# FFN-in linears of a two-block transformer kernel: the high weights against both activation halves in one 512-column matmul

## Chip, cores and metric

One core of a Trainium2 chip runs the whole program. The metric is the device time of one execution in microseconds.

## The reference

Two stacked blocks on a sequence of 256 tokens with width 1024 in float32. The first block has two layers, and each layer has two SwiGLU feed-forward nets (four in all), with an attention between them:

```
mod = c_act @ ada_w[layer] + ada_b[layer]
h = modulate(rms_norm(x, norm_g[layer, 0]), sh1, sc1)
x = x + 0.5 * g1[:, None, :] * swiglu(h, ffn_w_in[layer, 0], ffn_w_out[layer, 0])
```

`swiglu` multiplies h by a matrix of 1024 x 5632, takes silu of one half of the result times the other half, and multiplies that (hidden width 2816) by a matrix of 2816 x 1024. The modulation vectors `mod` come from matrices of their own, 1024 x 9216 a layer. The second block has convolution mixers, a cross attention and a gather of expert rows (PEER).

## The kernel before, in words

**Three matmuls for one product.** TensorE works on float32r operands. To keep float32 accuracy every weight tile and every activation is split into a high half and a low half, and a product is high x high + high x low + low x high. For a block of 128 output features and each of 8 input chunks k, `product` (L801) issues three matmuls of 256 columns (the tokens) into one PSUM bank: w_hi with HH, w_hi with HL, w_lo with HH. HH and HL are the activation's halves; the linears of f01_in read EH and EL.

**Weight tiles.** A weight tile is 1024 x 256, 1 MB, two blocks of 128 features. SP loads it into `raw`, a ring of three (L610; it waits until the low half of the tile three before has been made, L601). ScalarE copies it to `w_hi` (`split`, L1302: it waits for the load and for TensorE's end of the tile three before). VectorE makes `w_lo` = raw - w_hi (`split`, L1865). TensorE waits for the low half of a tile (L810) before the tile.

**An FFN.** The in-stage (f00_in, f01_in, f10_in, f11_in) has 22 tiles; the two blocks of tile t are the gate and the up half of hidden chunk t. ScalarE takes Silu of the first from PSUM (L1422), VectorE multiplies it by the second from PSUM (L1986) into `graw`, ScalarE copies that to `GUH` (high half, L1425) and GpSimd subtracts to `GUL` (low half, L711). The out-stage has 16 tiles of 1408 columns of weights, two for each of 8 feature blocks: 33 matmuls each. The first out-tile waits for hidden chunks 0 to 10, the second for all 22 (`hidden_lo`, L933).

**Order of work.** Each engine's program is written out by hand, slot by slot (a slot is one tile), with semaphores between them. 18 tiles of an in-stage are a loop of three passes over six tiles, the last ones are written out. In f01_in and f11_in the first two tiles are done ahead by another path (`raw_tile`), so that the loop begins at tile 2. The first tile of the stage waits for the activation's halves chunk by chunk; in `feat_tile` this is the branch `new` (L825 to L841), and since the branch is taken by the slot's number inside the loop, it is run in each of the three passes. The rest of the tiles take `product`.

**What shares the engines.** In f00, f01 and f10 VectorE also computes the modulation vectors (`mod_tile`, L1872: two scalar_tensor_tensor of 1024 with an accumulator over a 1 MB tile in `mod_ring`, a ring of two): in the in-stage in slots 0, 1, 3 and 4 of each six and in the last slots (18 to 21 counted from the loop's first tile, as far as they exist), then once per feature block of the out-stage. ScalarE's queue issues their loads (`load_mod`, L1316 and on), each after the tile two before has been eaten. f11 has no modulation tiles.

The slot of VectorE before: modulation tile, split of tile t+2, multiply of tile t. The slot of ScalarE before: load of a modulation tile, Silu of t, GUH copy of t, split of tile t+3. PSUM has six banks in turn for the outputs, three tiles.

## Time and profile before

| | us |
|---|---|
| median of 3 runs | 2137.27 |
| lowest, highest | 2137.02, 2140.35 |
| profiled execution, span | 2138.9 |
| TensorE busy (matmuls) | 1807.5, 85% |
| TensorE weight loads | 1552.8, 73% |
| VectorE busy | 1717.7, 80% |
| ScalarE busy | 860.6, 40% |
| GpSimd busy | 534.6, 25% |
| DMA mean | 283 GB/s |

The profiled execution has no time of its own beside its span; the span is 1.6 us over the median of the runs. The busy shares are averages over stages with different limits. Of the span the four FFNs take the stretches 45 to 240, 367 to 560, 607 to 801 and 892 to 1084; from 1512 on the PEER gather runs. TensorE's clock is given as a share of 2.4 GHz. Matmul ends in the profile are modelled, so that a matmul of 0.28 us follows the one before it after 0.12.

### The profile page before, as it was taken

Reading aid. Unit: us, or ns where it says so; the run is one execution under the profiler, and the core shown is the slowest. Engines: PE = TensorE matmul, PEld = TensorE weight load, DVE = VectorE, ACT = ScalarE, POOL = GpSimd, SP = SyncE. Lnnn points to the kernel's source line nnn. Section 1 sums busy time; section 2 is a strip of 40 time slices with the busy share of each in tenths; the row PEclk is TensorE's granted clock in tenths of the full one; section 3 lists DMA queues with packets and bytes.
Section 4 is the critical chain, followed back from the end, with each engine's and each line's share of the span. In section 5 each row is a group of like instructions: output and inputs, shape, how many; then the busy total and the mean of one; then the engine's idle time right before and its main releaser. Section 6 shows DMA issues by size and latency. Waiting matters only on the chain.

```text
span 2138.9 us, 32220 instructions
## 1 busy us (share of the span) xinstructions
PE 1807.5 (85%) x12184; PEld 1552.8 (73%) x12184; DVE 1717.7 (80%) x2974; ACT 860.6 (40%) x1352; POOL 534.6 (25%) x464
## 2 busy tenths in 40 slices
PE   4999898999999998999999999999655654566555
PEld 4999898999999997899999999989322221222222
DVE  5887777878887878654579998848999998999877
ACT  3443466544455446644444545555212111211101
POOL 0110002111001110211110002422556545445441
PEclk7999999999999998999999999999878777667776
DMA  7889733688868884254544454526999999999996
GB/s 317 316 318 366 293 121 141 255 313 295 293 245 310 303 312 173 99 200 169 167 174 168 177 179 167 197 99 273 412 422 422 422 423 421 422 423 423 422 423 264
DMA packets 88788, 606.34 MB, mean 283 GB/s; under 512 B 9763, under 2 KB 11059, under 8 KB 21468
## 3 DMA queue, kind: packets, MB, share of 16 engines
q1 hardware_dynamic: 37708, 245.03, 31.9%
q0 software_dynamic: 37040, 270.57, 30.4%
q10 hardware_dynamic: 13920, 89.15, 10.4%
q8 instruction: 75, 1.23, 0.2%
q14 instruction: 45, 0.37, 0.1%
HBM read 601.53 MB, written 3.18 MB: 283 GB/s over the span
## 4 chain that ended last, share of the span: by engine, by line
PE 24%; DVE 16%; DMA 15%; issue 3%; ACT 2%; POOL 1%; DVEq 0%; ACTq 0%; POOLq 0%
PE ps L806 16%; DMA row_pair<-in_peer_uv,mod_ring 15%; DVE row_pair L2527 3%; PE ps L1288 3%; DVE w_lo L1869 3%; DVE XTOK L2546 3%; PE ps L837 2%; DVE work L2297 2%; DVE SQ L2297 2%; POOL row_pair L778 1%; PE ps L869 1%; DVE work L1926 1%; PE ps L903 0%; DVE work L2499 0%; PE ps L1007 0%
## 5 line engine op out<-in xcount | busy, mean ns | idle before, releaser
L1869 DVE TENSOR_TENSOR w_lo<-raw,w_hi 128x2048 fp32r<-128x2048 f32 (+1 forms) x248 | 527.0, 2127 | 204.7 <-ACT w_hi L1310 204.5
L1288 PE MATMUL ps<-row_pair,diag 128*128 128x512 f32 x512 | 362.8, 875 | 259.0 <-ACT diag L1836 259.0
L1310 ACT ACTIVATE w_hi<-raw 128x2048 fp32r<-128x2048 f32 (+1 forms) x248 | 440.1, 1775 | 228.0 <-PE ps L806 160.8
L1288 PEld LDWEIGHTS ps<-row_pair,diag 128*128 128x128 f32 x512 | 139.4, 286 | 481.8 <-ACT diag L1836 312.5
L806 PE MATMUL ps<-HH,w_hi 128*128 128x256 f32 x1584 | 446.4, 282 | 0.0
L806 PE MATMUL ps<-HL,w_hi 128*128 128x256 f32 x1584 | 443.5, 280 | 0.0
L806 PE MATMUL ps<-HH,w_lo 128*128 128x256 f32 x1584 | 443.0, 280 | 0.0
L778 POOL DMA_INDIRECT row_pair<-in_peer_uv,mod_ring x256 | 324.8, 1269 | 326.5 <-PE ps L1288 227.1
L2527 DVE SCALAR_TENSOR_TENSOR row_pair<-row_pair,HTOK 128x1024 f32<-128x1024 f32 x256 | 311.7, 1218 | 61.8 <-DMA row_pair<-in_peer_uv,mod_ring 59.3
L806 PEld LDWEIGHTS ps<-HL,w_hi 128*128 128x128 f32 x1584 | 298.1, 188 | 0.7 <-issue 0.7
L806 PEld LDWEIGHTS ps<-HH,w_lo 128*128 128x128 f32 x1584 | 297.8, 188 | 0.0
L806 PEld LDWEIGHTS ps<-HH,w_hi 128*128 128x128 f32 x1584 | 296.8, 187 | 1.0 <-issue 0.7
L711 POOL TENSOR_TENSOR GUL<-work,GUH 128x256 f32 (+1 forms) x88 | 80.9, 919 | 542.5 <-ACT GUH L1425 502.1
L1886 DVE SCALAR_TENSOR_TENSOR mod_ring<-mod_ring,mod_acc 128x1024 f32<-128x1024 f32 x144 | 193.2, 1378 | 17.4 <-DMA mod_ring<-in_ada 16.5
L806 PE MATMUL ps<-GUH,w_hi 128*128 128x256 f32 x704 | 200.1, 284 | 3.2 <-DVE w_lo L1869 3.2
L806 PE MATMUL ps<-GUH,w_lo 128*128 128x256 f32 x704 | 199.9, 284 | 0.0
L806 PE MATMUL ps<-GUL,w_hi 128*128 128x256 f32 x704 | 199.9, 284 | 0.0
L1849 ACT ACTIVATE mod_ring<-mod_ring 128x4 f32<-128x4 f32 (+1 forms) x66 | 13.5, 205 | 398.2 <-DVE row_pair L2527 398.1
L806 PE MATMUL ps<-EH,w_hi 128*128 128x256 f32 x560 | 159.6, 285 | 5.4 <-POOL EL L684 2.9
L2546 DVE SCALAR_TENSOR_TENSOR XTOK<-row_pair,mod_ring,XTOK 128x1024 f32<-128x1024 f32 x126 | 161.2, 1279 | 0.0
L806 PE MATMUL ps<-EL,w_hi 128*128 128x256 f32 x560 | 159.4, 285 | 0.0
L806 PE MATMUL ps<-EH,w_lo 128*128 128x256 f32 x560 | 158.4, 283 | 0.0
(326 smaller groups left out, 3265.1 us busy)
## 6 DMA issues: line engine op xcount, KB each, us to landing
raw<-in_f_in SPq DMA_DIRECT2D x88, 1024.0 KB, 4.9
mod_ring<-in_ada ACTq DMA_DIRECT2D x74, 1024.0 KB, 7.1
raw<-in_f_out SPq DMA_DIRECT2D x64, 704.0 KB, 5.3
raw<-in_mix_a SPq DMA_DIRECT2D x16, 1024.0 KB, 4.9
raw<-in_mix_g SPq DMA_DIRECT2D x8, 1024.0 KB, 4.9
raw<-in_pq SPq DMA_DIRECT2D x8, 1024.0 KB, 6.0
first<-in_ada ACTq DMA_DIRECT2D x4, 1024.0 KB, 12.8
raw<-in_a_q SPq DMA_DIRECT2D x4, 1024.0 KB, 6.0
```

The lines of the kernel that those rows point to most:

```text
L711: nc.gpsimd.tensor_tensor(lo, graw[:, j % 2, :], f32(hi), ALU.subtract).then_inc(hidden_lo, 1)
L778: pool.indirect_dma_start(out=row_pair[n % ROW_SLOTS][:, :], out_offset=None, in_=a["peer_uv"], in_offset=bass.IndirectOffsetOnAxis(ap=IDX ...
L806: ins = mm(out_, ops[1] if left else ops[0], ops[0] if left else ops[1], start=(first and k == k0 and n == 0), stop=(last and k == k1 - 1 ...
L837: last = mm(ps[:, BANK[q], 0:SEQ], w[u][:, k, m * P:(m + 1) * P], src[part][:, k, :], start=(part == 0 and k == 0 and u == 0), stop=(part ...
L869: mm(outs[m], w[u][:, k, m * P:(m + 1) * P], hi[:, k, 0:wide], start=(k == 0 and u == 0), stop=False)
L1288: last = mm(ps[:, 2 * t + c, :], diag[:, d, :], row_v(k)[:, c * 512:(c + 1) * 512], start=False, stop=False)
L1310: f(slot(w_hi, g), slot(raw, g), ACT.Copy).then_inc(hi_ready, 1)
L1869: v.tensor_tensor(slot(w_lo, g), slot(raw, g), f32(slot(w_hi, g)), ALU.subtract).then_inc(low["v"], 1)
L1886: ins = v.scalar_tensor_tensor(w[:, j, :], w[:, j, :], 1.0, c_row, ALU.mult, ALU.mult, accum_out=mod_dot[:, n // 2 % 2, m:m + 1])
L2297: ins = v.scalar_tensor_tensor(dst, x, w31, dst, ALU.mult, ALU.add)
L2527: v.scalar_tensor_tensor(row_u(n), row_u(n), 1.0, HTOK[:, n // SLOTS_PER_TILE, :], ALU.mult, ALU.mult, accum_out=DOT[:, n:n + 1]).then_inc ...
L2546: ins = v.scalar_tensor_tensor(y, row_v(n), CF[:, n:n + 1], y, ALU.mult, ALU.add)
```

## The change

In the four FFN-in linears, outside the `new` branch, the high weights are multiplied with both halves of the activation in one matmul: the moving operand is a pair of 256 columns from HH and HL (now the two halves of one placed buffer `HHL`, at the same addresses; EH and EL likewise in `EHL`), and the output is a whole bank of 512 columns. The low weights times the high half go to columns 0 to 255. The sum of the bank's two halves, which PSUM made before, is now made by others: ScalarE copies columns 256 to 511 of both banks of the tile to `halves` (one ACTIVATE of 512), and VectorE adds that to columns 0 to 255 of both banks (one tensor_tensor of 512) into `gated`. Silu and the multiply then work in SBUF, in place. The slots are reordered. The `new` branch puts its low-half matmuls into columns 256 to 511, with as many matmuls as before.

```diff
 feat_tile (TensorE), new branch:
+                            cols = slice(SEQ, 2 * SEQ) if wide and part else slice(0, SEQ)
-                                    last = mm(ps[:, BANK[q], 0:SEQ], w[u][:, k, m * P:(m + 1) * P], src[part][:, k, :],
+                                    last = mm(ps[:, BANK[q], cols], w[u][:, k, m * P:(m + 1) * P], src[part][:, k, :],
...
 feat_tile, the other tiles:
+                    if wide:
+                        pair = ps[:, BANK[q], :].rearrange("p (a n) -> p a n", a=2)
+                        for k in range(DC):
+                            mm(pair, w[0][:, k, m * P:(m + 1) * P], both[:, :, k * SEQ:(k + 1) * SEQ], start=(k == 0), stop=False)
+                            last = mm(ps[:, BANK[q], 0:SEQ], w[1][:, k, m * P:(m + 1) * P], src[0][:, k, :],
+                                      start=False, stop=(k == DC - 1))
+                        last.then_inc(units_done, 1)
+                        continue
...
 ScalarE, slot_:
+                    act.wait_ge(units_done, at(i, 2 * BODY, CHUNK_UNIT[q + 1]))
+                    f(halves, ps[:, BANK[q]:BANK[q] + 2, SEQ:2 * SEQ], ACT.Copy).then_inc(half_copied, 1)
+                    act.wait_ge(halves_added, at(i, BODY, done + 1))
+                    f(gated[:, t % 2, 0, :], gated[:, t % 2, 0, :], ACT.Silu).then_inc(freed["a"], 1)
+                    if t < 21:
+                        split(ln.tile0 + t + 3, i)
                     if more and t - t0 in (1, 2, 4, 5, 19, 20, 21):
                         k = {1: 0, 2: 1, 4: 2, 5: 3, 19: 12, 20: 13, 21: 14}[t - t0]
                         load_mod(ada + k + 2, i)
-                    q = ln.chunk0 + 2 * t
-                    act.wait_ge(units_done, at(i, 2 * BODY, CHUNK_UNIT[q]))
-
-                    act.wait_ge(freed["d"], at(i, BODY, FREE[q + 1][1] - 2))
-                    f(silu[:, t % 2, :], ps[:, BANK[q], 0:SEQ], ACT.Silu).then_inc(freed["a"], 1)
                     act.wait_ge(freed["d"], at(i, BODY, FREE[q + 1][1]))
                     dst = GUH[:, t, :] if i is None else GUH[:, bass.ds(i * BODY + t, 1), :].rearrange("p a n -> p (a n)")
-                    f(dst, graw[:, t % 2, :], ACT.Copy).then_inc(hidden_hi, 1)
-                    split(ln.tile0 + t + 3, i)
+                    f(dst, gated[:, t % 2, 1, :], ACT.Copy).then_inc(hidden_hi, 1)
+                    if t == 21:
+                        split(ln.tile0 + t + 3, i)
...
 VectorE, slot_:
+                    if t == t0:
+                        split(ln.tile0 + t + 2, i)
+                    dve.wait_ge(half_copied, at(i, BODY, done + 1))
+                    dve.wait_ge(hidden_lo, at(i, BODY, FC * n + t + 1))
+                    v.tensor_tensor(gated[:, t % 2, :, :], ps[:, BANK[q - 1]:BANK[q - 1] + 2, 0:SEQ], halves, ALU.add
+                                    ).then_inc(halves_added, 1)
+                    if t0 < t < 21:
+                        split(ln.tile0 + t + 2, i)
+                    dve.wait_ge(freed["a"], at(i, BODY, FREE[q - 1][1]))
+                    v.tensor_tensor(gated[:, t % 2, 1, :], gated[:, t % 2, 1, :], gated[:, t % 2, 0, :], ALU.mult
+                                    ).then_inc(freed["d"], 1)
+                    if t == 21:
+                        split(ln.tile0 + t + 2, i)
                     if acc is not None:
                         mod_tile(ada + acc, i)
-                    split(ln.tile0 + t + 2, i)
                     if got is not None:
                         mod_take(ada // 2 + got, i)
-                    q = ln.chunk0 + 2 * t + 1
-                    dve.wait_ge(units_done, at(i, 2 * BODY, CHUNK_UNIT[q]))
-                    dve.wait_ge(freed["a"], at(i, BODY, FREE[q - 1][1]))
-
-                    dve.wait_ge(hidden_lo, at(i, BODY, FC * n + t + 1))
-                    v.tensor_tensor(graw[:, t % 2, :], ps[:, BANK[q], 0:SEQ], silu[:, t % 2, :], ALU.mult
-                                    ).then_inc(freed["d"], 1)
```

The GpSimd subtract and the two raw tiles of f01_in and f11_in read or write `gated` in the place of `graw` and `silu`, and are otherwise as before.

## Rows read from the trace of the kernel before

**Rows 1.** Busy time by stretch: f00_in, f00_out, f01_in, f11_in (PE, PEld, DVE, ACT, POOL, clock, DMA share, GB/s)
```profile
57.00:171.00 114.00, 114.00 (x969) 114.00 (x969) 95.19 (x110) 54.47 (x65) 19.13 (x21) 1.00 0.83 319
171.00:239.50 68.50, 65.34 (x530) 65.00 (x530) 48.88 (x61) 27.10 (x26) 6.62 (x6) 0.98 0.97 374
380.00:496.00 116.00, 116.00 (x964) 116.00 (x963) 95.80 (x110) 52.79 (x64) 19.57 (x21) 1.00 0.75 283
...
904.00:1020.00 116.00, 116.00 (x972) 115.58 (x971) 58.57 (x51) 55.79 (x73) 16.96 (x21) 1.00 0.51 176
```

**Rows 2.** The chain of waits in f11_in and behind it: start, us, what
```profile
909.80 28.26 PE ps L806 x240
...
1017.94 68.99 PE ps L806 x576
```

**Rows 3.** Timeline of VectorE in f00_in, one slot and a half
```profile
83.52 0.42 DVE L1986 TENSOR_TENSOR work<-ps,work 128x256 f32<-128x256 f32 x1
83.85 1.22 DVE L1886 SCALAR_TENSOR_TENSOR mod_ring<-mod_ring,mod_acc 128x1024 f32<-128x1024 f32 x1
...
84.99 1.76 DVE L1886 SCALAR_TENSOR_TENSOR mod_ring<-mod_ring,mod_acc 128x1024 f32<-128x1024 f32 x1
...
86.69 2.28 DVE L1869 TENSOR_TENSOR w_lo<-raw,w_hi 128x2048 fp32r<-128x2048 f32 x1
88.89 0.41 DVE L1986 TENSOR_TENSOR work<-ps,work 128x256 f32<-128x256 f32 x1
```

**Rows 4.** Timeline of ScalarE in the same slots
```profile
84.06 0.42 ACT L1425 ACTIVATE GUH<-work 128x256 f32 x1 [2.59 <-DVE work L1986]
...
86.30 1.28 ACT L1422 ACT_TABLE_LOAD   x1
87.59 0.39 ACT L1422 ACTIVATE work<-ps 128x256 f32<-128x256 f32 x1
```

**Rows 5.** Timeline of GpSimd in the same slots
```profile
84.66 1.01 POOL L711 TENSOR_TENSOR GUL<-work,GUH 128x256 f32 x1 [4.34 <-ACT GUH L1425]
```

**Rows 6.** Timeline at the end of f00_in: VectorE, ScalarE's queue, TensorE's first out-matmul
```profile
167.66 1.23 DVE L1886 SCALAR_TENSOR_TENSOR mod_ring<-mod_ring,mod_acc 128x1024 f32<-128x1024 f32 x1 [1.61 <-DMA mod_ring<-in_ada]
...
171.49 0.41 DVE L1986 TENSOR_TENSOR work<-ps,work 128x256 f32<-128x256 f32 x1
...
175.11 3.21 DVE L1869 TENSOR_TENSOR w_lo<-raw,w_hi 128x1408 fp32r<-128x1408 f32 x2
...
160.52 0.34 ACTq L1322 DMA_DIRECT2D mod_ring<-in_ada  x1
...
171.07 0.28 PE L806 MATMUL ps<-GUH,w_hi 128*128 128x256 f32 x1
```

**Rows 7.** Costliest groups by form: operations with 512 elements a partition (busy us, mean ns)
```profile
L1280 PE MATMUL ps<-XTOK,ident 128*128 128x512 f32 x8 | 3.6, 592 | 0.0
...
L2115 DVE TENSOR_TENSOR work<-work,rscale 128x512 f32<-128x512 f32 x12 | 8.0, 684 | 0.1
...
L1808 ACT ACTIVATE XTOK<-ps 128x512 f32<-128x512 f32 x4 | 2.2, 595 | 0.1
```

**Rows 8.** The chain of waits: fp32 matmuls of 256 columns and of one
```profile
1093.88 3.47 PE ps L903 x16
...
1452.20 1.23 PE ps L1265 x12
```

**Rows 9.** Busy time by stretch, line 806 alone: f01_in reads EH and EL, f11_in HH and HL
```profile
421.00:449.00 28.00, 28.00 (x234) 28.00 (x233) 1.00 0.83 322
910.00:937.00 27.00, 27.00 (x232) 27.00 (x231) 1.00 0.58 212
```

**Rows 10.** Timeline of TensorE in f00_out
```profile
222.09 0.38 PE L806 MATMUL ps<-GUH,w_hi 128*128 128x256 f32 x1 [3.16 <-DVE w_lo L1869]
```

**Rows 11.** Busy time by stretch, right after that (TensorE clock 0.50)
```profile
222.90:226.20 3.30, 3.30 (x18) 3.30 (x17) 2.17 (x4) 0.00 (x0) 0.00 (x0) 0.50 0.97 402
```

**Rows 12.** DMA issues of the page: KB each, median us to landing
```profile
raw<-in_f_in SPq DMA_DIRECT2D x88, 1024.0 KB, 4.9
```

More of the change, by code:

```diff
@@ L49 @@
 DIRECT = 3
+FFN_IN = ("f00_in", "f01_in", "f10_in", "f11_in")
+WIDE_BEFORE = (0, 22, 42, 64)
 MOD_L0, MOD_KV, MOD_L1 = 0, 72, 88
@@ L287, in build_program @@
         mod_ring = place("mod_ring", MOD_AT, 2 * TILE)
-        HH = three(place("HH", HH_AT, DC * SEQ, F32R), DC)
-        HL = three(place("HL", HL_AT, DC * SEQ, F32R), DC)
+        HHL = place("HHL", HH_AT, 2 * EXT, F32R)[:, :].rearrange("p (a n) -> p a n", a=2)
+        HH = HHL[:, 0, 0:DC * SEQ].rearrange("p (a b) -> p a b", a=DC)
+        HL = HHL[:, 1, 0:DC * SEQ].rearrange("p (a b) -> p a b", a=DC)
         SQ = three(place("SQ", SQ_AT, DC * SEQ), DC)
@@ L293, in build_program @@
         bias = KS
-        EH = three(place("EH", KS_AT, DC * SEQ, F32R), DC)
+        EHL = place("EHL", KS_AT, 2 * EXT, F32R)[:, :].rearrange("p (a n) -> p a n", a=2)
+        EH = EHL[:, 0, 0:DC * SEQ].rearrange("p (a b) -> p a b", a=DC)
         KL = EH
@@ L299, in build_program @@
         VS = three(place("VS", VS_AT, TT * D), TT)
-        EL = three(place("EL", VS_AT, DC * SEQ, F32R), DC)
+        EL = EHL[:, 1, 0:DC * SEQ].rearrange("p (a b) -> p a b", a=DC)
         SUBR = three(place("SUBR", VS_AT, DC * SEQ), DC)
@@ L358, in wk @@
             return v
-        silu = wk(2 * FC * SEQ, 512, 2, SEQ)
-        graw = wk(2 * FC * SEQ + 512, 512, 2, SEQ)
+        gated = wk(2 * FC * SEQ, 1024, 2, 2, SEQ)
+        halves = wk(13320, 512, 2, SEQ)
         HEADS = A_HEADS // 2
@@ L515, in build_program @@
         hl_ready = sem("hl_ready")
+        half_copied = sem("half_copied")
+        halves_added = sem("halves_added")
         hidden_hi = sem("hidden_hi")
@@ L710, in one @@
                         lo, hi = (g_[:, bass.ds(i * BODY + j, 1), :].rearrange("p a n -> p (a n)") for g_ in (GUL, GUH))
-                    nc.gpsimd.tensor_tensor(lo, graw[:, j % 2, :], f32(hi), ALU.subtract).then_inc(hidden_lo, 1)
+                    nc.gpsimd.tensor_tensor(lo, gated[:, j % 2, 1, :], f32(hi), ALU.subtract).then_inc(hidden_lo, 1)
                 with pool.Fori(0, 3) as i:
@@ L824, in feat_tile @@
                 src = (EH, EL) if second else [p_[:, :, 0:SEQ] for p_ in RAWS[N_PEER]] if name == "pq" else (HH, HL)
+                wide = name in FFN_IN
+                both = EHL if second else HHL
                 if new is not None and t == (RAW_TILES if raw else 0):
@@ L836, in feat_tile @@
                                 for u in range(2 - part):
-                                    last = mm(ps[:, BANK[q], 0:SEQ], w[u][:, k, m * P:(m + 1) * P], src[part][:, k, :],
-                                              start=(part == 0 and k == 0 and u == 0), stop=(part == 1 and k == DC - 1))
+                                    last = mm(ps[:, BANK[q], cols], w[u][:, k, m * P:(m + 1) * P], src[part][:, k, :],
+                                              start=((part == 0 or wide) and k == 0 and u == 0),
+                                              stop=((part == 1 or (wide and u == 1)) and k == DC - 1))
                             if part == 1:
@@ L1413, in slot_ @@
                 def slot_(t, i=None):
+                    q = ln.chunk0 + 2 * t
+                    done = WIDE_BEFORE[n] + t - t0
+                    act.wait_ge(units_done, at(i, 2 * BODY, CHUNK_UNIT[q + 1]))
[4 more added lines that the diff above has]
+                        split(ln.tile0 + t + 3, i)
                     if more and t - t0 in (1, 2, 4, 5, 19, 20, 21):
@@ L1434, in ffn @@
                         act.wait_ge(freed["d"], FREE[q + 1][1] - 2)
-                        f(silu[:, t % 2, :], TX[:, 2 * t, 0:SEQ], ACT.Silu, bias=TX[:, 2 * t, SEQ:SEQ + 1]).then_inc(freed["a"], 1)
+                        f(gated[:, t % 2, 0, :], TX[:, 2 * t, 0:SEQ], ACT.Silu, bias=TX[:, 2 * t, SEQ:SEQ + 1]).then_inc(freed["a"], 1)
                         act.wait_ge(freed["d"], FREE[q + 1][1])
-                        f(GUH[:, t, :], graw[:, t % 2, :], ACT.Copy).then_inc(hidden_hi, 1)
+                        f(GUH[:, t, :], gated[:, t % 2, 1, :], ACT.Copy).then_inc(hidden_hi, 1)
                 else:
@@ L1975, in slot_ @@
                     got = {2: 0, 5: 1, 20: 6}.get(t - t0) if more else None
+                    q = ln.chunk0 + 2 * t + 1
+                    done = WIDE_BEFORE[n] + t - t0
+                    if t == t0:
[11 more added lines that the diff above has]
+                        split(ln.tile0 + t + 2, i)
                     if acc is not None:
                         mod_tile(ada + acc, i)
-                    split(ln.tile0 + t + 2, i)
                     if got is not None:
                         mod_take(ada // 2 + got, i)
-                    q = ln.chunk0 + 2 * t + 1
-                    dve.wait_ge(units_done, at(i, 2 * BODY, CHUNK_UNIT[q]))
-                    dve.wait_ge(freed["a"], at(i, BODY, FREE[q - 1][1]))
-                    dve.wait_ge(hidden_lo, at(i, BODY, FC * n + t + 1))
-                    v.tensor_tensor(graw[:, t % 2, :], ps[:, BANK[q], 0:SEQ], silu[:, t % 2, :], ALU.mult
-                                    ).then_inc(freed["d"], 1)
                 if raw:
```

2 lines of the change are left out of this document (1 added, 1 removed).

## The prediction, made before the changed kernel ran

> **What bounds the kernel now.** I read the stretches first [rows 1]. TensorE is busy for the whole of each FFN-in stage at full clock (114 of 114 us, 116 of 116), so today TensorE sets the pace there. VectorE comes next: 95.19 of 114 us in f00_in and 95.80 of 116 in f01_in, but only 58.57 of 116 in f11_in, which has no modulation tiles between its weight tiles. In f00_out the DMA engines are 0.97 busy. The chain of waits then gives TensorE's pace [rows 2]: 240 matmuls in 28.26 us, 0.1178 us each, so a weight tile of 48 takes 5.65 us. The 48 at L837 are the first tile of each pass of the loop of six. That line is inside the loop body, so it runs three times in a stage, and the change leaves its 48 narrow matmuls as they are. Next the timelines of VectorE, ScalarE and GpSimd [rows 3 to 5] show what has to fit beside 5.65 us, and those of the stage's end [rows 6] what is queued there.
>
> **1. TensorE.** A feature block of 128 now costs, for each k, three 256-column matmuls, 0.353 us. Afterwards it is one of 512 and one of 256. No fp32r matmul of 512 columns is in the trace. The fp32 ones are: eight of 512 took 3.6 us with the last one's 0.59 of latency, so (3.6-0.59)/7 = 0.43 us each [rows 7]; sixteen of 256 took 3.47 us, 0.217 each [rows 8]. Cost there is in proportion to columns, with next to nothing fixed, and half of it is 0.215 and 0.108. The fp32r matmul of 256 takes 0.1178 and not 0.108; twelve one-column matmuls still take 1.23 us, 0.10 each [rows 8], so I read a floor of 0.10 to 0.12 as the weight load. Behind a 512 the load is hidden, behind a 256 it is not: 0.215+0.1178 = 0.333. Ends: 0.215+0.108 = 0.323 below; 3x0.1178 = 0.353 above (the 0.1178 goes by columns), and 3% over that, since the stage that reads EH and EL gets 234 matmuls into 28 us where HH and HL get 232 into 27 [rows 9], so that where the moving data lies costs 3%. I take 0.333. A changed tile falls from 5.65 to 16x0.333 = 5.33, by 0.33 us. Changed are 22-3 = 19 tiles in f00_in and f10_in, 20-3 = 17 in f01_in and f11_in: 72 tiles, 24 us if TensorE sets the pace everywhere.
>
> By the Trainium skill (TensorE: Matmul & The Clock Gate, "Back-to-back issue gap") 256 columns take 262 cycles and 512 take 518, so the pair would take an estimated 0.325 us. This trace disagrees for 256 (0.1178 against 0.109); by the page f11_in would gain an estimated 7.7 us and the whole come to 2143.
>
> **2. VectorE, between the weight tiles.** Now, per tile: split 2.20 (86.69 to the multiply after it), multiply 0.33 (83.52 to 83.85) and, in two slots of three, a modulation tile of 2.84 (83.85 to 86.69) [rows 3]. Three slots: 6.6+1.0+5.7 = 13.3 us of 16.95. Each slot gets an add of 512 elements. Nearest row: TENSOR_TENSOR of 512, 0.684 us [rows 7]; less the 0.08 by which the next one overlaps it, 0.61 (ends 0.5 and 0.8). The multiply loses its PSUM operand and I leave it at 0.33.
> Beside the adds, 1.8 us per three slots, three waits appear:
> - GpSimd's GUL subtract starts 1.14 us after the multiply (83.52 to 84.66) and takes 1.01; the modulation half beside it takes 1.76 instead of 1.22 [rows 3, 5]. Behind the third multiply of three there is no modulation tile and afterwards the next add and split follow, so the split pays the 0.54 that is paid by a modulation tile now or falls into idle time: +0.5 (0 if it misses).
> - The Silu's table load, 1.28 us, comes in the first slot of each pass in f00_in and f10_in [rows 4]. It is hidden now. Afterwards it lies between add and multiply, and in exactly that slot the split stands ahead of the add: VectorE idles 1.28+0.39 [rows 4] and a handoff, 1.7 us a pass, 0.85 per three slots.
> - With VectorE late and no modulation tile behind the multiply, the next add waits for multiply, GUH copy (starts 0.54 after the multiply, takes 0.42 [rows 4]) and half copy (0.59 by the PSUM copy of 512 [rows 7]) in a row: about 1.1 us idle.
> Sum: 13.3+1.8+0.5+0.85+0.6 to 1.1 = 17.1 to 17.6, against 16.95 now and 16.0 for TensorE. Going through the queues slot by slot, part of it overlaps: a pass of six comes to 34.1 in f00_in and f10_in (34.0 now) and 32.8 in f01_in (no table load in the loop). So with modulation tiles the TensorE gain is mostly gone. The stage starts with some lead and ends 1.7 us earlier in f00_in and f10_in, 3.8 in f01_in, to which I add 2.8 because today its 17 tiles run 3% slower. In f11_in nothing binds (3.2 us a slot): -17x0.33 = -5.7.
>
> By the Trainium skill (GPSIMD Engine Reference, "1. Specifications") GpSimd contends with a VectorE instruction of two SBUF inputs. The trace agrees for the modulation tiles (1.76 against 1.22); whether the multiply, which becomes such an instruction, is hit too no row shows (third rival; by the row's 0.54 it would be 2156).
>
> **3. The end of the in-stage.** The last four slots of f00_in and f10_in each have a modulation tile, and the order turns: now modulation, split, multiply; afterwards add, split, multiply, modulation, and in the last slot the split of the second out-tile comes behind the multiply. Today multiply 21 starts at 171.49, 0.4 us after TensorE ends the tile at about 171.07, and the splits of out-tiles 2 and 3 follow at 175.11 [rows 6], in time for 171.07+2x3.96 (33 matmuls of 0.12; the chain's 576 in 68.99 [rows 2]). Afterwards VectorE enters slot 21 some 2.2 us late, as four slots of 5.98 meet tiles of 5.33. Counted from the end E of TensorE's tile: multiply at E+4.3, split of out-tile 1 done at E+6.3 (1.62 long), where TensorE wants it at E+3.96: stall 2.4. Then modulation 15 (2.84), gate and take (0.3), modulation 16 (2.84; its load can only be issued after modulation 14 and took 7.1 us from issue to use, 160.52 to 167.66 [rows 6]), split of out-tile 2 done at E+14.9 against E+10.4: stall 4.6. Together 7.0, less 1.7: **+5.4 in f10 and f00 each**. For f00 I take off 2, since its out-stage is DMA-bound (0.97) and held TensorE 3.16 us at 222 anyway [rows 1, 10]; this is a guess between 0 and 5. f01 has modulation in the last two slots and the first out-slot: stalls 1.2+4.6, less 3.8 and 2.8: **-0.8**. In f11 the chain copy, add, Silu, multiply, GUH, GUL takes 4.05 of a cover of 3.96: 0.2, so **-5.5**.
> After an idle of 3.16 us the clock was at half for a stretch (18 matmuls in 3.3 us at 0.50 of the clock, which is 1.2 GHz of 2.4 [rows 11]), which costs 1.7 us; stalls of 4.6 in three stages: **+5.1**.
>
> **4. Costed at nothing.** SP's weight loads are issued when a split frees its slot, 4.9 us to landing [rows 12], and the split comes earlier in its slot than now. ACT gets 0.6 more a slot and has 40% of the span busy; its order (Silu, split, GUH) no longer has the split behind the multiply. Modulation loads are issued from ACT up to 3 us later and land before use except at the end, which is in part 3. If the loads take 0.6 us more, three tails cost 1.8. PSUM: banks come free by Silu and multiply three tiles ahead, 10 us of room. GpSimd idles.
>
> **Sum.** 3.4+5.4-0.8-5.5+5.1 = +7.6. The profiled execution's span of 2138.9 would become 2146.5; it stands 1.6 over the median, so on the median 2137.3+7.6 = 2145.
>
> **Rivals.**
> - *VectorE keeps up* (faster). If the GUL subtract misses the splits and the adds take 0.5, three slots cost VectorE 15.5 to 16.0 and TensorE sets the pace: -24 in the four stages. The tails stay with their last four slots: +7.0+7.0+4, less what a shorter lag saves (-3), and one half-clock stretch instead of three (+1.7), gives -7: 2130. The point is 16.0 us for three slots. For it: the trace has VectorE idle for 17% of f00_in. Against: the sums of part 2. 0.27.
> - *The wide matmul costs two narrow ones*, 0.353. f11 gains nothing and the tails stay; the pace with modulation tiles is then slowed by both sides: 2145+5.5+4 = 2155. Fp32's proportional cost is for it, the one-column floor against. 0.15.
> - *The table load or the handoffs weigh twice*, or the multiply is hit by GpSimd's subtract: +0.5 on 64 slots is 32 us at most, and I take a third of it: 2156. 0.08.
> - *Nothing much changes*: smaller stalls (loads ready, clock not falling) but no gain: 2137. 0.15.
> - My forecast, 2138 to 2151: 0.35.
>
> **Numbers.** A change within 0.2% (4.3 us) can't be told from none. Faster by more: 0.25, nearly all the first rival. Within: 0.22, the fourth rival and the edges of the first and of the forecast. Slower: 0.53. The range of 8 in 10 reaches from the first rival to the third: 2128 to 2160.
>
> **What would show it.** In f11_in tiles of 5.33 us and a stage 5 to 6 us shorter (5.16: weight load hidden too; 5.65: second rival). In f00_in and f10_in tiles of 5.6 to 5.7 with TensorE waiting for VectorE's w_lo, and VectorE near 0.97 busy; if TensorE never waits there, the first rival holds. At the start of f00_out, f01_out and f10_out two waits of TensorE for w_lo of about 2 and 4.6 us and a half-clock stretch behind the second. The add at 0.69 us, the half copy at 0.59, a table load between add and Silu. The prediction is wrong as a whole if TensorE runs through the changes from in to out without a wait: then the result is near 2115.

## The result, and the profile after

| | before | after |
|---|---|---|
| median | 2138.15 us (12 runs beside those of after) | 2144.19 us (12 runs) |
| ratio to before, 95% interval | | 1.0029 [1.0021, 1.0036] |
| profiled execution's span | 2138.9 us | 2147.7 us |

Slower by 6 us, 0.29%, as forecast. The two profiled executions differ by 8.8 us, more than the medians do: the profiled one of the changed kernel (2149.5 us) was the slowest of its twelve. First the eight stretches of the changed kernel by engine: the four in-stages, then the four out-stages (the numbers in brackets count instructions).

```profile
core 0: us, PE busy (x) PEld busy (x) DVE busy (x) ACT busy (x) POOL busy (x), PEclk, DMA share, GB/s
45.06:170.10 125.04, 124.69 (x753) 111.39 (x753) 113.88 (x146) 78.84 (x98) 22.58 (x21) 0.99 0.79 290
385.74:498.00 112.26, 112.26 (x691) 100.38 (x689) 99.76 (x122) 65.48 (x82) 23.33 (x21) 1.00 0.77 285
617.79:741.90 124.11, 124.11 (x753) 111.64 (x754) 107.79 (x132) 79.31 (x95) 22.32 (x21) 0.99 0.75 276
915.77:1030.66 114.89, 114.89 (x706) 103.32 (x705) 67.51 (x69) 68.75 (x91) 19.50 (x21) 1.00 0.48 172
170.10:244.06 73.96, 67.29 (x531) 66.51 (x529) 54.38 (x69) 27.99 (x28) 8.35 (x7) 0.95 0.98 372
498.00:566.02 68.02, 65.15 (x530) 64.77 (x529) 55.12 (x76) 31.02 (x36) 8.71 (x6) 0.97 0.89 317
741.90:811.24 69.34, 65.31 (x531) 64.93 (x530) 53.45 (x69) 28.13 (x28) 11.10 (x7) 0.98 0.89 316
1030.66:1094.82 64.16, 63.57 (x531) 63.40 (x530) 39.90 (x43) 31.11 (x37) 11.18 (x6) 1.00 0.58 195
```

The length of each, by the starts of TensorE's matmuls, beside the same stretch of before:

| stretch | before | after | difference | forecast |
|---|---|---|---|---|
| f00_in, f10_in | 126.5, 126.1 | 125.0, 124.1 | -1.5, -2.0 | -1.7 each |
| f01_in | 115.8 | 112.3 | -3.6 | -6.6 |
| f11_in | 116.7 | 114.9 | -1.8 | -5.7 |
| f00_out | 68.4 | 74.0 | +5.5 | +6.7 |
| f01_out | 63.4 | 68.0 | +4.7 | +7.5 |
| f10_out | 63.4 | 69.3 | +6.0 | +8.7 |
| f11_out | 63.4 | 64.2 | +0.8 | +0.2 |

The last column collects the prediction's terms by place. The change gives 8.8 us in the in-stages and loses 17.0 behind them: +8.2 of the 8.8. Not all of that is the change: the run with Silu's table loaded ahead has the same out-stages instruction for instruction, and in its profile f00_out took 71.2 us and f01_out 66.7, where 74.0 and 68.0 stand here.

**In the in-stages TensorE still sets the pace.** In the first view it is busy for the whole of three of them and for all but 0.35 us of f00_in. What it waited for within f00_in (TensorE's waits, 44 to 171 us; the 13 us are the start of the stage, ahead of its first matmul):

```profile
PE ps L846 <- ACT HHL L1392: 13.0, 1, 13.0
PE ps L860 <- DVE w_lo L1891: 0.3, 1, 0.3
```

VectorE's queue held it once, for 0.35 us, at the second tile. The gain per tile is small because the wide matmul is dear. Five changed tiles, 80 wide matmuls, took 27.73 us in f11_in and 28.02 in f01_in, 5.55 and 5.60 us a tile (the stretches from the first of them to the next narrow one, the wide matmuls and their weight loads alone):

```profile
921.49:949.22 27.73, 27.73 (x80) 14.91 (x80) 1.00 0.54 193
391.42:419.44 28.02, 28.02 (x80) 14.90 (x80) 1.00 0.74 269
```

From start to start a matmul of 512 columns takes 0.231 us and the one of 256 behind it 0.1166: 0.3475 for the pair, against 0.353 for three narrow ones. In f01_in the narrow ones took 5.81 us a tile, so there the pair gives more, 0.21 a tile. With 19, 17, 19 and 17 tiles: 0.106x19 = 2.0, 0.21x17 = 3.6, 2.0, 0.106x17 = 1.8. The stages show 1.5, 3.6, 2.0 and 1.8.

**Behind them TensorE waits twice in three of the four stages.** TensorE's waits from 165 to 820 us (total, times, longest), those in the out-stages. Before had only the one of [rows 10], in f00_out; the fourth wait for `w_lo` here, 2.0 us at 234.6 in the same stage, is in its place:

```profile
PE ps L812 <- DVE w_lo L1891: 10.5, 4, 3.4
...
PE ps L812 <- POOL GUL L717: 3.1, 3, 1.2
```

At 754.21 us, in f10_out, TensorE starts the third tile 2.79 us late. VectorE's timeline up to it (start, duration, in brackets the idle time before and who ended it):

```profile
743.39 0.68 DVE L2004 TENSOR_TENSOR work<-ps,work 128x512 f32<-128x512 f32 x1
744.55 0.42 DVE L2009 TENSOR_TENSOR work<-work 128x256 f32<-128x256 f32 x1 [0.48 <-ACT work L1438]
744.89 1.62 DVE L1891 TENSOR_TENSOR w_lo<-raw,w_hi 128x1408 fp32r<-128x1408 f32 x1
746.43 1.75 DVE L1908 SCALAR_TENSOR_TENSOR mod_ring<-mod_ring,mod_acc 128x1024 f32<-128x1024 f32 x1
...
749.25 0.16 DVE L2044 TENSOR_SCALAR half_gate<-mods 128x8 f32<-128x8 f32 x1
...
750.24 1.23 DVE L1908 SCALAR_TENSOR_TENSOR mod_ring<-mod_ring,mod_acc 128x1024 f32<-128x1024 f32 x1 [0.62 <-DMA mod_ring<-in_ada]
...
752.53 3.16 DVE L1891 TENSOR_TENSOR w_lo<-raw,w_hi 128x1408 fp32r<-128x1408 f32 x2
```

The in-stage ended at 741.90. Addition, multiply, split of the second out-tile, modulation tile 15, the gate, tile 16 and then the third tile's split stand in a row, in the order that part 3 of the prediction wrote down; before, modulation tile 15 and the split of the second tile were ahead of the multiply. The first of the two waits, 1.2 us at 747.24, is for GUL and not for `w_lo`: GpSimd began the last slice at 745.50, inside the split of 744.89, and took 1.59 us for it, where a slice with nothing of two SBUF operands beside it takes 0.74. The split itself was done at 746.51, so without the slice TensorE would have waited for it, some 0.6 us (0.57 in the run with the late wait). Behind the second the clock fell:

```profile
754.20:757.60 3.40, 3.39 (x17) 0.55 0.89 327
```

17 matmuls in 3.4 us, 0.55 of the full clock, so mostly at 1.2 GHz of 2.4. The Trainium skill (TensorE: Matmul & The Clock Gate, "What's actually happening") sets the clock by how busy the engine has lately been; the trace agrees. The length of a wait doesn't settle it, though. In f01_out the second wait was 2.28 us in this kernel, in the one with two narrow matmuls and in the one with Silu's table loaded ahead. Behind it the clock was 0.56 here (509.2 to 512.6) and 1.00 in the other two, and the stage took 68.0 us here and 66.7 there.

### The profile page after: what moved, and what is told of

The parts are those of the page before. It is cut to its first block, busy times and chain, and to the rows that moved or that the text cites. A ratio compares the mean times of both kernels' runs of the same rounds, so it can differ in the third digit from the quotient of the medians.

```text
span 2147.7 us, 30024 instructions
## 1 busy us (share of the span) xinstructions
PE 1807.2 (84%) x11032; PEld 1498.6 (70%) x11032; DVE 1762.6 (82%) x3058; ACT 927.0 (43%) x1442; POOL 550.0 (26%) x464
## 4 chain that ended last, share of the span: by engine, by line
PE 23%; DVE 16%; DMA 16%; issue 3%; ACT 2%; POOL 1%; DVEq 0%; POOLq 0%; ACTq 0%
DMA row_pair<-in_peer_uv,mod_ring 16%; PE ps L812 10%; DVE row_pair L2556 3%; PE ps L860 3%; DVE w_lo L1891 3%; PE ps L1306 3%; PE ps L846 2%; DVE XTOK L2575 2%; DVE work L2326 2%; DVE SQ L2326 2%; PE ps L861 1%; POOL row_pair L784 1%; PE ps L887 1%; DVE work L1948 1%; PE ps L921 0%
## 5 line engine op out<-in xcount | busy, mean ns | idle before, releaser
L860 PE MATMUL ps<-HHL,w_hi 128*128 128x512 f32 x880 | 306.3, 393 | 0.3 <-DVE w_lo L1891 0.3
L812 PE MATMUL ps<-HHL,w_hi 128*128 128x256 f32 x1408 | 253.3, 281 | 0.6 <-DVE w_lo L1891 0.5
L861 PE MATMUL ps<-HHL,w_lo 128*128 128x256 f32 x880 | 246.2, 280 | 0.0
L717 POOL TENSOR_TENSOR GUL<-work,GUH 128x256 f32 (+1 forms) x88 | 94.9, 1078 | 530.0 <-ACT GUH L1446 489.6
L812 PEld LDWEIGHTS ps<-HHL,w_hi 128*128 128x128 f32 x1408 | 215.6, 188 | 2.8 <-issue 1.4
L812 PE MATMUL ps<-HHL,w_lo 128*128 128x256 f32 x704 | 196.7, 279 | 0.0
L860 PEld LDWEIGHTS ps<-HHL,w_hi 128*128 128x128 f32 x880 | 165.2, 188 | 36.9 <-issue 0.5
L861 PEld LDWEIGHTS ps<-HHL,w_lo 128*128 128x128 f32 x880 | 166.2, 189 | 0.0
L812 PEld LDWEIGHTS ps<-GUH,w_hi 128*128 128x128 f32 x704 | 137.9, 196 | 16.0 <-DVE w_lo L1891 15.9
L812 PEld LDWEIGHTS ps<-GUL,w_hi 128*128 128x128 f32 x704 | 138.0, 196 | 0.0
```

What stands on the lines that cost most here:

```text
L717: nc.gpsimd.tensor_tensor(lo, gated[:, j % 2, 1, :], f32(hi), ALU.subtract).then_inc(hidden_lo, 1)
L812: ins = mm(out_, ops[1] if left else ops[0], ops[0] if left else ops[1], start=(first and k == k0 and n == 0), stop=(last and k == k1 - 1 ...
L860: mm(pair, w[0][:, k, m * P:(m + 1) * P], both[:, :, k * SEQ:(k + 1) * SEQ], start=(k == 0), stop=False)
L861: last = mm(ps[:, BANK[q], 0:SEQ], w[1][:, k, m * P:(m + 1) * P], src[0][:, k, :], start=False, stop=(k == DC - 1))
```

## Experiments

Each is an edit of the changed kernel, but for the first and the fourth. Times are medians. A ratio is to runs of the kernel before on the same chip.

### The wide matmul alone

The kernel before with this in the in-stages, the halves side by side in memory, and nothing else:

```
+ for k in range(DC):
+     mm(pair, w[0][...], both[:, :, k * SEQ:(k + 1) * SEQ], start=(k == 0), stop=False)
+     last = mm(ps[:, BANK[q], 0:SEQ], w[1][...], src[0][:, k, :], ...)
```

> The kernel before with the wide matmul alone: the 512-column and the 256-column matmul of the changed kernel, the halves laid side by side, and no copy, no addition and the slot order of before. The half of each bank that holds high weights times low activations is left out of the result. Theory (the in-stages are bound by TensorE in every stage, and what the change loses it loses in the tail behind them): the in-stages give the same as in the changed kernel, f00_in -1.5, f01_in -3.5, f10_in -2.0, f11_in -1.8 us, the out-stages stay at 63.4 and 68.4 us, the total is 9 us under before: 2129. Rival (a queue holds the in-stages: VectorE's 4.5 us of modulation work or the weight ring, and the addition hides behind it): the out-stages give part of it back without the addition too, total 2133 to 2138.

2128.8 us, ratio 0.9952 [0.9935, 0.9969]: 10 us faster, with the low half's share left out of the result. Its out-stages took 65.3, 63.4, 63.5 and 63.4 us: the stalls are not the wide matmul's doing. f10_in took 122.6 us, 1.5 less than the theory's 124.1; that turned out to be the clock (last section). The 10 us also hold some of f00_out, 3.1 us shorter in the profile than before.

### Two narrow matmuls in place of the wide one

```
- mm(pair, w[0][...], both[:, :, k * SEQ:(k + 1) * SEQ], start=(k == 0), ...)
+ for h in range(2):
+     mm(pair[:, h, :], w[0][...], src[h][:, k, :], start=(k == 0 and h == 0), ...)
```

> The changed kernel with its 512-column matmul taken apart into two of 256 columns, into the same two halves of the bank; copy, addition and order are kept. Theory (TensorE sets the pace of the in-stages, pair 0.3475 us against 0.353): the 72 tiles cost 0.066 us each more, 4.8 us, and up to the 8.9 us that the in-stages had gained; the stalls behind them shrink a little since VectorE gets more time: 2149 to 2153. Rival (VectorE's queue sets the pace, the matmul's saving is hidden): no change, 2144.

2156.0 us, 1.0080 [1.0063, 1.0098]: 12 us over the changed kernel, in the theory's direction but past its 5 to 9. Its stretches can't say where the rest is, since the profiled execution (span 2150.8) was the fastest of its runs. From the end of f00_out to the start of f01_out it took 256.65 us, the kernel before 256.68 and the changed one 253.94; f10_in and f11_in too are back at 126.1 and 116.7. So at the old pace, with copy and addition in place, the stages are as long as before, and the in-stage's gain is TensorE's alone. The out-stages keep their loss (72.3, 66.7, 70.2, 64.2).

### The third split moved ahead

```
                     if t == 21:
                         split(ln.tile0 + t + 2, i)
+                        split(ln.tile0 + t + 3, i)
```
(and it leaves the loop of the out-stage)

> The changed kernel with one step moved: VectorE's split of the third out-stage tile is issued right behind the last in-stage split, ahead of modulation tiles 15 and 16. Theory (the waits of TensorE on w_lo at 183.01, 509.16 and 754.21 us are this split standing behind two modulation tiles; 3.4 + 2.3 + 2.8 us, with 3 x 1.2 to 1.7 us of low clock behind them): those waits vanish, 2131 to 2134, under both kernels. Rival (the split waits for its weight tile's transfer, or the next one in the queue is late in its place): 2140 to 2144.

2144.0 us, 1.0021 [1.0008, 1.0034]: the rival. The wait didn't go, it moved two tiles on, from the third tile (behind 66 matmuls of the stage) to the fifth (behind 132). In f10_out TensorE and VectorE:

```profile
759.37 0.39 PE L812 MATMUL ps<-GUH,w_hi 128*128 128x256 f32 x1 [3.04 <-DVE w_lo L1891]
```
```profile
755.40 1.22 DVE L1908 SCALAR_TENSOR_TENSOR mod_ring<-mod_ring,mod_acc 128x1024 f32<-128x1024 f32 x1 [3.02 <-DMA mod_ring<-in_ada]
...
757.70 3.15 DVE L1891 TENSOR_TENSOR w_lo<-raw,w_hi 128x1408 fp32r<-128x1408 f32 x2
```

VectorE stands idle for 3.02 us ahead of a modulation tile, and the split of the fifth out-tile is behind that tile. The tile's load was issued at 747.89 and landed 7.5 us later, and it was issued that late because its half of the ring (two tiles) held modulation tile 15 until 747.8. So the chain is: a modulation tile eaten late, the load two tiles on issued late, a split queued behind it.

### The new order alone

The kernel before with its slots in the changed order (split behind the wait for the matmuls, modulation tile behind the multiply, ScalarE's split behind Silu); three narrow matmuls, no copy, no addition.

```
+ if t == t0: split(...)
  dve.wait_ge(units_done, ...)
+ if t0 < t < 21: split(...)
  v.tensor_tensor(graw, ps, silu, ALU.mult)
+ if t == 21: split(...)
+ mod_tile(...); mod_take(...)
```

> The kernel before with the changed kernel's order alone: VectorE splits the weight tile behind its wait for the matmuls, the modulation tile comes behind the multiply, ScalarE waits for both chunks ahead of Silu and splits behind it; three narrow matmuls, no copy and no addition. Theory (the order alone puts the split behind the last multiply and both modulation tiles ahead of the out-stage's third split): in-stages unchanged, waits of about 1 to 1.5 us at the three switches, total 2139 to 2143, that is about half of the loss. Rival (the loss is the queue lag from the addition's 0.69 us and the handoffs): 2137 to 2139.

2147.1 us, 1.0040 [1.0025, 1.0055]: +8, more than either expected. Second waits of 2.7, 1.8 and 1.6 us, f01_out 66.9, f10_out 65.2, and 2 us more in f00_in. Those 2 us are no wait: in f00_in each narrow matmul took 0.120 us from start to start where before it took 0.1178, and in f10_in, from the same operands, 0.1178 again. Why is open. With the first run: wide matmul -10, order +8. If these add up, copy and addition on top cost the rest, about 8; no run has them alone (2144.2 against 2138.9-10.1+8.2 = 2137.0, and the two-narrow kernel's 2156.0 against this one's 2147.1 give 7 and 9).

### The modulation tiles ahead again

VectorE's `mod_tile` and ScalarE's `load_mod` back at the head of their slots; the splits stay.

```
+ if acc is not None: mod_tile(ada + acc, i)
  if t == t0: split(...)
+ if got is not None: mod_take(...)
  dve.wait_ge(half_copied, ...)
```

> The changed kernel with the modulation tiles back at the head of their slots, on VectorE (ahead of the wait for the copy) and their loads on ScalarE (ahead of the copy); the splits stay where the change put them. New theory (after moving the third split cured nothing, 2144): the stalls come from a chain, a modulation tile eaten late, its ring half loaded late (ScalarE issues that load only then, and has its own split behind it), the load landing 5 to 8 us later, and a split of VectorE or ScalarE queued behind that. With the tiles eaten 3 to 5 us sooner in slots 18 to 21 the second stalls of 3.4, 2.3 and 2.8 us go: 2134 to 2138. Rival (the splits' new place behind the last multiply, or the addition's time on VectorE, makes the stalls): 2142 to 2146.

2141.4 us, 1.0015 [1.0006, 1.0024]: 3 us better, not 6 to 10. The second stall is gone in all three stages, as the theory says, but the first one grew: modulation tile 15 now delays addition, multiply and with them GUL. Waits of TensorE in f10_out, 738 to 812 us:

```profile
PE ps L812 <- POOL GUL L717: 2.7, 1, 2.7
```

### The splits ahead, and the whole old order with the addition

The first puts VectorE's split at the head of each slot, ahead of the wait for the copy; the second the modulation tile as well, as before the change.

```
+ split(ln.tile0 + t + 2, i)
  dve.wait_ge(half_copied, ...)
  v.tensor_tensor(gated, ps, halves, ALU.add)
- if t0 < t < 21: split(...)
  dve.wait_ge(freed["a"], ...)
```

> The changed kernel with VectorE's splits back at the head of every slot, ahead of the wait for the copy; the modulation tiles stay at the back. Theory of the modulation chain: little is gained, only the first stall's part in the three out-stages (1.2, 0.6, 1.2 us, each the GUL subtraction behind the last multiply), 2142 to 2145. Rival (place of the splits): the stalls go, 2134 to 2138. Against both: splits ahead of the addition may delay it, and with it the release of the banks, so that the in-stages lengthen.

> The changed kernel with VectorE's whole old order (modulation tile, split, sum, then the waits, the addition and the multiply) and ScalarE's modulation loads back ahead of the copy: wide matmul, copy and addition stay. Theory (the loss is the order's 8 us, the wide matmul gives 10 and the addition's own 0.69 us a tile costs the rest): 2133 to 2138, below the changed kernel by 6 to 10. Rival (the addition and the copy themselves make the stalls, whatever the order): 2143 to 2147.

2177.5 us, 1.0188 [1.0174, 1.0202], and 2189.1 us, 1.0248 [1.0232, 1.0263]. Both theories missed: the old order can't carry the addition. With the splits ahead TensorE waits for `w_lo` nine times in f00_in (45 to 165 us), 5.3 us in all, so there VectorE does set the pace. Lines of VectorE's groups, 80 to 165 us, first of the changed kernel, then with the splits ahead:

```profile
L1891 DVE TENSOR_TENSOR w_lo<-raw,w_hi 128x2048 fp32r<-128x2048 f32 x15 | 34.2, 2278 | 0.0
L2004 DVE TENSOR_TENSOR work<-ps,work 128x512 f32<-128x512 f32 x15 | 10.3, 685 | 6.3 <-ACT work L1436 6.3
L2009 DVE TENSOR_TENSOR work<-work 128x256 f32<-128x256 f32 x15 | 6.2, 416 | 2.1 <-ACT work L1438 2.1
```
```profile
L1891 DVE TENSOR_TENSOR w_lo<-raw,w_hi 128x2048 fp32r<-128x2048 f32 x15 | 39.7, 2644 | 6.5 <-ACT w_hi L1328 6.5
L2003 DVE TENSOR_TENSOR work<-ps,work 128x512 f32<-128x512 f32 x14 | 9.5, 681 | 0.0
L2006 DVE TENSOR_TENSOR work<-work 128x256 f32<-128x256 f32 x14 | 6.0, 425 | 7.9 <-ACT work L1438 7.9
```

Three things differ. The split no longer lies between addition and multiply, so VectorE idles through Silu each time: 7.9 us in 14 slots, 0.56 each, where it was 2.1. It waits for ScalarE's high half, which stands behind that Silu: 6.5 us in all. And it costs 2.64 us on average instead of 2.28, because GpSimd's GUL subtraction is now already running when the split starts. GpSimd and VectorE at 94 to 98 us:

```profile
95.74 1.03 POOL L717 TENSOR_TENSOR GUL<-work,GUH 128x256 f32 x1 [3.32 <-ACT GUH L1446]
```
```profile
96.11 2.82 DVE L1891 TENSOR_TENSOR w_lo<-raw,w_hi 128x2048 fp32r<-128x2048 f32 x1
```

The split pays 0.54 us, which is the 0.5 of the prediction's part 2. In the changed kernel the same two meet the other way round, the split starting first (85.68 us), and then GpSimd pays:

```profile
86.41 2.14 POOL L717 TENSOR_TENSOR GUL<-work,GUH 128x256 f32 x1 [4.96 <-ACT GUH L1446]
```
```profile
85.68 2.28 DVE L1891 TENSOR_TENSOR w_lo<-raw,w_hi 128x2048 fp32r<-128x2048 f32 x1
```

That is part of why the addition fits in only with the changed order. The 1.03 of the earlier pair is itself more than a lone slice's 0.74: that slice began inside a half of a modulation tile (94.96 to 96.18) and waited for its end. In the changed kernel 57 of the 88 slices begin inside a split or such a half, and each ends 0.58 to 0.60 us after it; the others take 0.74. The Trainium skill (SBUF — State Buffer, "SBUF: two separate sides") says that whichever of the two starts first keeps the port pair for its whole instruction and the other blocks; the trace agrees, by these 0.58 to 0.60 us.

### Silu's table loaded ahead

One Silu on one column ahead of the loops of f00_in and f10_in.

```
                 split(ln.tile0 + 2)
+                preload(ACT.Silu)
             with act.Fori(0, 3) as i:
```

> The changed kernel with one more activation of Silu on one column ahead of the loops of f00_in and f10_in. Theory (the loop's body starts from an unknown table, hence two table loads of 1.28 us a pass in these stages and none in f01_in and f11_in): both loads vanish from the passes and ScalarE saves 15 us, but the in-stages are bound by TensorE, so the time stays: 2143 to 2145. Rival (the table loads between addition and Silu delay VectorE, as I forecast): 2 to 4 us faster, 2140 to 2142.

2144.1 us, 1.0032 [1.0019, 1.0045], no change. In the changed kernel each pass had two table loads in f00_in (ScalarE's groups, 45 to 170 us):

```profile
L1436 ACT ACT_TABLE_LOAD x3 | 3.8, 1283 | 0.1
L1438 ACT ACT_TABLE_LOAD x3 | 3.8, 1283 | 0.1
```

Here both are gone from the passes. The load ahead of Silu did hold VectorE, as forecast (idle 1.04 us ahead of the multiply at 89.90), but VectorE has that much to spare: in the 85 us (15 slots) of its groups shown above it stood idle for 6.3 us until ScalarE's copy, which itself waits for TensorE.

### The wait for the last GUL slice made late, alone and with the modulation ahead

TensorE waited for all 22 slices ahead of the second out-tile, though only its last three matmuls read the last.

```
- pe.wait_ge(hidden_lo, 2 + FC * f + WO_K * (half + 1))
+ pe.wait_ge(hidden_lo, 2 + FC * f + WO_K * (half + 1) - (1 if t == 1 else 0))
+ ... all matmuls but the last slice's
+ if t == 1: pe.wait_ge(hidden_lo, 2 + FC * f + FC)
```

> The changed kernel with the late wait for the last GUL slice alone. Theory (TensorE reaches the third tile earlier by the first stall, and there waits for the same split behind the same modulation tiles): the 1.2 us move into the second stall, f01_out, f10_out keep 68 and 69, f11_out, which has no modulation, gives back its 0.8: 2143 to 2144. Rival (the first stalls cost by themselves): 2139 to 2141.

2144.9 us, 1.0027 [1.0018, 1.0037]: alone it gives nothing. f11_out gives back 0.6 of its 0.8 us; in f00_out the second wait grew from 3.4 to 3.9, in f01_out from 2.3 to 2.9, in f10_out it stayed (2.8 and 2.7). In f00_out and f10_out 0.6 us of the first wait is left, now on the split of the second tile. The theory held in the main.

> The changed kernel with its modulation tiles at the head of their slots and, new, TensorE's wait for the last GUL slice moved from the head of the second out-stage tile to just ahead of that slice's three matmuls (30 matmuls, 3.6 us later). Theory (with the modulation ahead the second stall is gone and the multiply of slot 21 is what GUL and TensorE wait for, 2.75, 0.74, 2.73 and 0.59 us in the four out-stages): these go, with the low clock behind them, f01_out, f10_out and f11_out come back to 63.4, f00_out to 68 or 69: 2132 to 2136, now under the kernel before by 2 to 6. Rival (another wait takes their place, the split of the third tile or the modulation loads): 2138 to 2141.

2139.7 us, 1.0000 [0.9986, 1.0014]: level with the kernel before, and the rival was right that another wait would come. In f10_out GUL is off the list, and in its place:

```profile
PE ps L812 <- DVE w_lo L1896: 2.1, 1, 2.1
```

the split of the second tile, which ran from 741.94 to 743.5, behind modulation tile 15, addition and multiply.

### Slot 21 in another order

The last kernel, and on VectorE in slot 21 alone: split of the second out-tile, addition, multiply, modulation tile, split of the third.

```
+ if acc is not None and t < 21: mod_tile(ada + acc, i)
+ if t in (t0, 21): split(ln.tile0 + t + 2, i)
  ... addition, multiply
+ if acc is not None and t == 21: mod_tile(ada + acc, i)
+ if t == 21: split(ln.tile0 + t + 3, i)
```

> The changed kernel with the modulation ahead and the late GUL wait (as in the run before, 2139.7), and in slot 21 alone another order on VectorE: split of the second out-stage tile first, then addition and multiply, then the modulation tile, then the split of the third out-stage tile, which leaves the loop of the out-stage. Theory (what is left are waits for VectorE's queue at the switch: 2.1 us on the split of the second tile, which stood behind modulation tile, addition and multiply): f01_out comes to 63.4, f10_out to 63.4 to 64.5, f00_out to 69 or 70, total 2132 to 2136, below the kernel before by 3 to 6. Rival (each thing moved ahead makes the next one late; the modulation loads, which land 5 to 9 us after their issue, then hold the third or the fourth tile as they did when the third split alone was moved): 2138 to 2141, a stall of 1.5 to 3 us one tile later.

2133.8 us, 0.9976 [0.9966, 0.9986]: 4.2 us under the kernel before and 10 under the changed one. Of this 1.5 us is the clock at f10_in's start (last section) in the profiled executions, which no edit here touches. VectorE and the stretch of f10_out, which began at 734.18:

```profile
733.90 1.61 DVE L1896 TENSOR_TENSOR w_lo<-raw,w_hi 128x1408 fp32r<-128x1408 f32 x1
735.44 0.68 DVE L2013 TENSOR_TENSOR work<-ps,work 128x512 f32<-128x512 f32 x1
736.60 0.43 DVE L2018 TENSOR_TENSOR work<-work 128x256 f32<-128x256 f32 x1 [0.48 <-ACT work L1446]
...
739.77 1.62 DVE L1896 TENSOR_TENSOR w_lo<-raw,w_hi 128x1408 fp32r<-128x1408 f32 x1
```
```profile
734.18:797.53 63.35, 63.35 (x530) 63.35 (x529) 51.90 (x66) 28.35 (x29) 10.86 (x7) 1.00 0.91 335
```

The splits end at 735.5 and 741.4, ahead of TensorE's need (738.1 and 742.1, at 3.96 us a tile). f01_out, f10_out and f11_out take 63.35 us without a wait. f01_in took 113.5 us for 112.3, with a wait of 0.8 for `w_lo` at its second tile. Only f00_out stays long, 71.8 against 68.4 before, with its DMA engines at a share of 1.00. Three waits are left there, the longest 4.1 us on a `w_lo`; what order of transfers would cure them was not tried.

### The price of the matmul forms

```
  f00_in: mm(ps[:, BANK[q], :], w[0], both[:, 0, k_ * SEQ:(k_ + 2) * SEQ])   # k_ = min(k, 6)
  f10_in: mm(ps[:, BANK[q], 0:128], w[1], src[0][:, k, 0:128])
  f11_in: mm(pair, w[1], both[:, :, k * SEQ:(k + 1) * SEQ])
```

> The changed kernel with other forms of its in-stage matmuls, to time them: f00_in takes its 512 columns contiguous instead of as two runs of 256 (a wrong neighbour takes the low half's place), f10_in multiplies the low weights with 128 columns instead of 256, f11_in multiplies the low weights too with 512; f01_in as it was. Theory (a matmul costs its columns at 0.445 ns each and about 3 ns beside, hence 231 and 117 ns): contiguous 231, 128 columns 60, the second 512-column one 231. Rival (the two runs of 256 columns cost something, or a floor by the weight load of about 100 to 117 ns): contiguous 218, 128 columns 100 or more.

One execution, 2175.9 us; what it multiplies is partly something else than the kernel's operands. Medians from start to start. Contiguous 512 columns: 0.232 us, and five tiles in the same 27.73 us as in two runs of 256, so those cost nothing. The second wide matmul: 0.231; it makes a tile of f11_in 1.9 us longer, 33 us for 17 tiles, which is the whole of what this run loses on the changed kernel. With 128 columns the rival is right: the narrow one takes 0.057, but the wide one ahead of it 0.283 instead of 0.231, and the pair 0.340 where the theory has 0.291. Half the columns save only 0.008. Five tiles took 27.15 us against 27.73:

```profile
653.02:680.17 27.15, 27.15 (x80) 14.85 (x80) 1.00 0.85 314
```

## Why the prediction was right, and where it wasn't

The forecast was 2145.0, the measurement 2144.2. The sum came out (+7.6; the medians give +6.0, the stretches of the profiles +8.2) because two errors cancelled: gains 7 us too large, losses 6 too large. That the total is this near is luck.

- **Part 1, the wide matmul: mis-sized.** I took 0.215 for 512 columns from fp32's proportional cost, plus a weight load that a 512 hides; the run has 0.231, 7% more, twice the narrow one less 2%. So the second rival was nearer here: the pair is 0.3475, with 0.333 forecast and 0.353 for "costs two narrow ones", and 72 tiles bring 9 us, not 24. By the Trainium skill (TensorE: Matmul & The Clock Gate, "Back-to-back issue gap"), from its cycles for a matmul by itself, the estimate was 0.325; the trace disagrees for both sizes (0.1166 and 0.231 measured, 0.109 and 0.216 by the page). What was right is that an fp32r matmul has a floor: at 128 columns the pair hardly gets cheaper.
- **Part 2, VectorE binds: wrong, with the right number.** The pass of six takes 33.45 us, set by TensorE, where I had VectorE at 34.1. TensorE waited once in the in-stages, for 0.35 us, and the changed tile of 5.55 us leaves VectorE 0.2 more a slot than my 5.33. The step that failed is the sum of waits. The GUL collision (+0.5 on the split) isn't paid by VectorE in the new order: where GUL meets a split, the split started first and stays at 2.28 us. The run with the splits ahead shows that the term would have been real, and the stage bound by VectorE, in the other order. The handoffs were counted as idle time, but lie in slack, the 6.3 us of waits for the copy. The multiply, with both operands in SBUF now, keeps its 0.42 us (third rival). The first rival's premise, VectorE keeps up, held in all four stages; what it priced at -24 was worth 9. That f00_in and f10_in came out at -1.5 and -2.0 with -1.7 forecast is chance: another engine set it.
- **f01_in: half.** I took 3.8 from the lag and 2.8 for the 3%. It gave 3.6, 0.21 a tile: the wide pair is free of most of the 3%. That the 3% comes from where the data lies isn't shown: with the order alone f00_in, which reads HH and HL, took 5.77 us a tile.
- **Part 3, the end of the in-stage: right in its mechanism, and it decided the sign.** The order of the queue, the two waits, the late load and the clock behind them all stand in the trace. The sizes: first wait 1.2 for 2.4, and on GUL, since VectorE was only some 0.7 us late by slot 21 where I had 2.2 (in f10_in the copy was done 0.8 us after the in-stage's end, the addition began at 1.5 and the multiply at 2.65, for my 4.3); second 3.4, 2.3 and 2.8 for 4.6. The clock cost was about right for f01 and f10 (0.56 and 0.55 behind the wait), less in f00 (0.72); in f01 that was chance, since behind the same wait the clock stayed at 1.00 in two other kernels. f11_out lost 0.8 for the 0.2 forecast. Two of the sums slip by 0.1: 7.0 less 1.7 is 5.3, and 4.05 against 3.96 is 0.1.
- **Part 4: nothing hidden came to light** but two table loads a pass for one, which cost nothing.
- **Behind part 3** the runs show more than I had seen. The loss isn't the addition's 0.69 us alone. The order costs 8 us without it, of which some 5 are in f01_out and f10_out: it moves the last multiply, a split and the modulation ring's loads against each other, and in the runs here any one moved by itself made another one late. Moving three things together and the GUL wait freed the out-stages.

What stays open: how much of the last kernel's gain each of its three edits carries where they weren't run apart, and whether the late GUL wait or slot 21's order would help the kernel before.

## What to carry to other kernels

A wider matmul is worth what its start-to-start time says, not its column count: time the form in a stage that TensorE binds before building on it. When a change reorders an engine's queue, write the queue down past the end of the loop, up to the point where the other engines have caught up; there the slack that hides it in the loop is gone. A stall cured by moving one step tends to show up at the next step, so look at the trace after each move, not at the total only.

## What the runs showed of the hardware

- An fp32r matmul of 512 columns takes 0.230 to 0.232 us from start to start at full clock, in one run of memory or in two of 256; one of 256 takes 0.117 behind it; one of 128 delays its neighbour so that the pair falls only from 0.348 to 0.340.
- Of GpSimd's subtraction and a VectorE operation with two SBUF operands only the one that starts second is lengthened: the split 2.82 for 2.28 us, a modulation half 1.75 for 1.22, or GUL 0.97 to 2.14 (2.44 in the kernel with the splits ahead) for 0.74. GUL then ends 0.58 to 0.60 us after the operation it began in, however long that still ran. If VectorE's next one has two SBUF operands as well, it starts second in its turn and pays 0.53 or 0.54. VectorE's addition, with an operand in PSUM, keeps its 0.69.
- A loop on ScalarE whose body begins with Copy and goes on to Silu had two table loads of 1.28 us a pass; a Silu ahead of the loop removed both.
- The clock behind a wait isn't told by the wait. Behind 2.28 us in f01_out it was 0.56 in the changed kernel and 1.00 in two others. At f10_in's start it differed too, although TensorE's last idle time ahead of it was 2.0 us in all. The first 6 us of before and of the changed kernel ran at 0.72, those of the wide matmul alone and of the last kernel at 1.00:

```profile
611.34:617.34 6.00, 6.00 (x38) 0.72 0.00 0
```
```profile
603.68:609.68 6.00, 6.00 (x49) 1.00 0.01 3
```

That is worth 1.5 us (126.1 or 124.1 against 122.6 for the stage) and came with no edit that touches this place. A comparison of single profiles to better than 2 us needs this line beside it. What decides it is open.
